# Modulation vectors of a two-layer trunk: VectorE row sums over a transposed w_mod in place of matmuls in the heads

## The reference, cut to what matters

```
def trunk_layer(x, cond, layer, lp, rope, ctx):
    mod = cond @ lp['w_mod'] + lp['b_mod']          # cond (1, 1024), w_mod (1024, 6144)
    sh1, sc1, g1, sh2, sc2, g2 = jnp.split(mod[:, None, :], 6, axis=-1)
    hmix = rmsnorm(x, lp['norm1_g']) * (1 + sc1) + sh1
    mix, new_ctx = token_mixers(hmix, layer, lp, rope, ctx)
    x = x + g1 * mix
    hffn = rmsnorm(x, lp['norm2_g']) * (1 + sc2) + sh2
    gate, up = jnp.split(hffn @ lp['w_ffn_in'], 2, axis=-1)
    x = x + g2 * ((jax.nn.silu(gate) * up) @ lp['w_ffn_out'])
...
        ctx_cond = jax.nn.silu(c_ctx)[None, :]
        lat_cond = jax.nn.silu(c)
```

## Time and profile before

| | |
|---|---|
| three runs | 3978.43, 3982.35, 3986.39 us (median 3982.35) |
| the profiled execution | 3979.51 us; span of its instructions 3977.7 us |
| busy: PE, DVE, POOL, ACT | 86%, 36%, 36%, 21% of the span |
| mean granted TensorE clock | 0.916 of full speed |
| bytes moved | 242.62 MB, mean 61 GB/s |

### The profile page before, as it was taken

How to read it: one execution, slowest core, us unless ns; L and a number is a source line. 1 busy time by engine, 2 the same in 40 slices (tenths; PEclk the granted TensorE clock), 3 DMA queues, 4 the chain that set the end, 5 groups by cost and what they waited for, 6 DMA issues and landing times.

```text
span 3977.7 us, 55062 instructions
## 1 busy us (share of the span) xinstructions
PE 3424.3 (86%) x21792; PEld 3061.2 (77%) x21792; DVE 1432.8 (36%) x2231; ACT 817.8 (21%) x1639; POOL 1437.6 (36%) x1088
## 2 busy tenths in 40 slices
PE   6978887877889987999987888797688998799997
PEld 5967777546569987999977777684384898799996
DVE  2067773355432122111122667705553222211112
ACT  3133332232110112010022333313311111200001
POOL 0454442002215543444424444320040354344443
PEclk8989998877799998999988999997797999899999
DMA  4201112111112211222211111121120121122221
GB/s 163 75 33 43 43 43 75 56 43 51 49 39 75 75 64 53 70 76 70 77 60 58 43 43 45 52 67 44 44 77 28 53 75 64 53 75 69 70 75 69
DMA packets 62882, 242.62 MB, mean 61 GB/s; under 512 B 6961, under 2 KB 6961, under 8 KB 61489
## 3 DMA queue, kind: packets, MB, share of 16 engines
q1 hardware_dynamic: 60336, 224.77, 17.6%
q10 hardware_dynamic: 1728, 12.36, 0.8%
q0 software_dynamic: 576, 2.10, 0.2%
HBM read 234.48 MB, written 4.72 MB: 60 GB/s over the span
## 4 chain that ended last, share of the span: by engine, by line
PE 66%; issue 10%; DVE 9%; POOLq 5%; POOL 4%; ACT 2%; DVEq 2%; DMA 1%; ACTq 0%; SPq 0%
PE ps_G L582 27%; PE ps_GPM L582 26%; POOLq L2002 5%; PE ps_M L960 2%; POOL gu_hi L1985 1%; DVE small L1735 1%; PE ps_GPM L613 1%; PE ps_G L848 1%; POOL gu_lo L1985 1%; POOL big L2011 1%; PE ps_M L905 1%; PE ps_M L662 1%; DVE big L1766 1%; PE ps_M L988 1%; PE ps_M L887 1%
## 5 line engine op out<-in xcount | busy, mean ns | idle before, releaser
L1949 POOL CAST w_hi<-ring 128x1024 fp32r<-128x1024 f32 x296 | 310.1, 1048 | 1596.7 <-PE ps_G L582 983.8
L1951 POOL TENSOR_TENSOR w_lo<-ring,w_hi 128x1024 fp32r<-128x1024 f32 x296 | 740.9, 2503 | 51.8 <-issue 8.9
L582 PE MATMUL ps_G<-room_a,w_hi 128*128 128x320 f32 x1984 | 455.7, 319 | 92.6 <-DVEq L1434 61.9
L582 PE MATMUL ps_GPM<-room_a,w_hi 128*128 128x320 f32 x1984 | 437.5, 309 | 0.0
L582 PEld LDWEIGHTS ps_G<-room_a,w_hi 128*128 128x128 f32 x1984 | 346.4, 196 | 95.8 <-DVEq L1434 63.7
L582 PE MATMUL ps_G<-room_b,w_hi 128*128 128x320 f32 x1408 | 369.0, 315 | 24.0 <-DVEq L1434 24.0
L582 PE MATMUL ps_G<-room_o,w_hi 128*128 128x320 f32 x1280 | 337.4, 313 | 44.3 <-DVEq L1434 44.3
L582 PE MATMUL ps_GPM<-room_b,w_hi 128*128 128x320 f32 x1408 | 361.4, 309 | 0.0
L582 PE MATMUL ps_GPM<-room_o,w_hi 128*128 128x320 f32 x1280 | 332.9, 309 | 0.0
L582 PEld LDWEIGHTS ps_GPM<-room_a,w_hi 128*128 128x128 f32 x1984 | 331.9, 188 | 0.0
L2001 POOL TENSOR_TENSOR outs<-big,con 128x512 f32<-128x512 f32 x168 | 208.7, 1242 | 296.7 <-DVEq L1582 190.5
(11 more groups left out here) (392 smaller groups left out, 5941.4 us busy)
## 6 DMA issues: line engine op xcount, KB each, us to landing
ring<-in_W SPq DMA_DIRECT2D x416, 512.0 KB, 3.5
big<-in_INV ACTq DMA_DIRECT2D x2, 1664.0 KB, 6.8
par<-in_PARAMS ACTq DMA_DIRECT2D x2, 1646.0 KB, 8.9
big<-in_FWD ACTq DMA_DIRECT2D x2, 1632.0 KB, 8.0
x<-in_X SPq DMA_DIRECT2D x1, 2560.0 KB, 8.9
out_Y<-h SPq DMA_DIRECT2D x1, 2560.0 KB, 7.5
con<-in_CONSTS SPq DMA_DIRECT2D x1, 1364.0 KB, 11.7
sc<-in_HYCS ACTq DMA_DIRECT2D x2, 578.5 KB, 3.5
```

Of the source, the lines that this page charges most:

```text
L582: m = pe.matmul(ap, w[wi][:, k, n0:n0 + P], acts[ai][k][:, a:b], start=(k == 0 and i == 0), stop=(k == chunks - 1 and i == 2))
L1949: nc.gpsimd.tensor_copy(hi, raw)
L1951: nc.gpsimd.tensor_tensor(wlo[:, slot * UNIT:(slot + 1) * UNIT], raw, hi.bitcast(F32), ALU.subtract)
```

## The change

The host lays `w_mod` out transposed, as 48 tiles per layer of 128 channels x 1024 inputs (`WMOD`), and both conditions broadcast over the partitions (`COND`, 128x2x1024). ACT applies silu to the broadcast conditions. DVE then makes each tile's 128 channels for both conditions: two `scalar_tensor_tensor` over 128x1024 with a running sum (`accum_out`) along the row, a drain behind each (`mod_tile`). PE's modulation matmuls and turns, ACT's row copies and DVE's bias additions in the heads are gone, and the ring has 304 units in place of 416. Of layer 0, 16 tiles are made ahead of everything else and 32 beside `A`; layer 1's 48 tiles are made beside the `f1` iterations of layer 0's FFN, four or five in each of the 11 iterations. Layer 1 has no next layer, so 96 tiles are made in all.

```diff
+            def mod_tile(w, junk, layer, tile):
+                for q in range(2):
+                    stt(junk, w, 1.0, condv[:, q, :], ALU.mult, ALU.mult, accum_out=modl[:, layer, tile, q:q + 1])
+                    dve.drain()
+            def ring_tiles(tiles_):
+                for r in tiles_:
+                    layer, tile = mod_source(r)
+                    dve.wait_ge(mod_landed[r % MOD_BUFS], 16 * (r // MOD_BUFS + 1))
+                    mod_tile(mod_buffer(r), early_junk if r < EARLY else late_junk, layer, tile)
+                    dve.drain().then_inc(mod_used, 1)
...
-            first_groups, groups = FIRST_MOD // 4, 3 * H
-            for i in range(0, first_groups):
-                add_bias(i + 1, i * 4, cn("b_first")[:, bass.ds(i * 4, 4)])
+            dve.wait_ge(cond_ready, 1)
+            for g in range(4):
+                dve.wait_ge(first_in[g], 16)
+                for t in range(4 * g, 4 * g + 4):
+                    mod_tile(first_tiles[:, t, :], early_junk, 0, t)
...
                 dve.drain().then_inc(g_ready.sem, 1)
+                if L == 0:
+                    ring_tiles(range(EARLY))
+                    add_bias(0, FIRST_TILES, N_MOD, pr("b_mod"))
...
                         I = L * (FT // 2) + i + first // 2
+                        if L == 0:
+                            if I == 0:
+                                dve.wait_ge(cond_ready, 2)
+                            ring_tiles(late_tiles(I))
+                            if I == FT // 2 - 1:
+                                add_bias(1, 0, N_MOD, pr("b_next"))
                         dve.wait_ge(gate_silu, I + 1)
...
             # SP
+            for r in range(EARLY):
+                after.setdefault(2 + r * 13 // EARLY, []).append(r)
+            for i in range(FT // 2):
+                for r in late_tiles(i):
+                    after.setdefault(f1[4 * i + 2], []).append(r)
+            for n in range(DEPTH * UNITS):
+                if n >= RAW:
+                    sp.wait_ge(unit_used, n - RAW + 1)
+                sp.dma_start(rv[:, n % RAW, :], W[n]).then_inc(landed[n % RAW], 16)
...
+                for r in after.get(n, []):
+                    if r >= MOD_BUFS:
+                        sp.wait_ge(mod_used, r - MOD_BUFS + 1)
+                    l, t = mod_source(r)
+                    sp.dma_start(mod_buffer(r), WMOD[l, t]).then_inc(mod_landed[r % MOD_BUFS], 16)
...
             # PE
-                    mod_units("delta", (0, 1, 2, 3), L, hd)
...
-                        if step < 2:
-                            mod_units("delta", (4 + 2 * step, 5 + 2 * step), L, hd)
-                    pe.wait_ge(rows_delta.sem, rows_delta.at(Q, 2))
-                    fill("delta", "cols1", L, hd)
-                    turn_rows(mod_rows)
...
-                        mod_units("attn", (qb,), L, hd)
                         if qb:
                             transposed(qb - 1)
...
             # ACT
+            act.dma_start(par[:, :], PARAMS[0]).then_inc(par_in.sem, 16)
+            condition(1)
```

More of the change, by code:

```diff
@@ L115, in at @@
         bank, base, k, per = self.where[phase, name]
-        ahead = FIRST_FILLS if bank == "GP" else 0
-        return bank, layer * self.total[bank] + step * per + (ahead + base + k + 1)
+        return bank, layer * self.total[bank] + step * per + (base + k + 1)
 def tile_fills(prefix, tiles):
@@ L186 @@
 ]
-FIRST_FILLS = 2 * (FIRST_MOD // 4)
 TURNS = Turns(PLAN)
@@ L200, in at, with trunk_program @@
         return step * self.per + k
-def trunk_program(nc, W, PARAMS, CONSTS, ROPES, HYCS, FWD, INV, X, Y, KNEW, VNEW, SNEW):
+def trunk_program(nc, W, WMOD, COND, PARAMS, CONSTS, ROPES, HYCS, FWD, INV, X, Y, KNEW, VNEW, SNEW):
     ctx = ExitStack()
@@ L420, in trunk_program @@
         consts_in = sem("consts_in")
+        eps_ready = sem("eps_ready")
+        cond_in = sem("cond_in")
         cond_ready = sem("cond_ready")
[L422 to L425, removed]
+        first_in = [sem(f"first_mod_tiles_in_{g}") for g in range(4)]
+        mod_landed = [sem(f"mod_tile_landed_{s}") for s in range(MOD_BUFS)]
+        mod_used = sem("mod_tile_used")
         par_in = sig_("params_in", 16)
@@ L607, in products @@
                     tile_product(phase, f"{prefix}{t}", t, layer, step, w, 0, acts, chunks).then_inc(unit_used, 1)
[L609 to L630, removed]
             def sum_squares(phase, layer, src, k_count, wait):
@@ L1052, in tiles, with condition @@
                 return view[:, bass.ds(at, 1), a:b].rearrange("p a t -> p (a t)")
+            def condition(time):
+                act.wait_ge(cond_in, 16 * time)
+                nc.scalar.activation(condv, condv, ACT.Silu)
+                act.drain().then_inc(cond_ready, 1)
+            act.dma_start(par[:, :], PARAMS[0]).then_inc(par_in.sem, 16)
+            condition(1)
             act.wait_ge(consts_in, 32)
@@ L1058, in _ @@
             act.drain()
[L1059 to L1067, removed]
             def squares(tiles_):
@@ L1436, in _, with add_bias @@
             htiles = [hv[:, k, :] for k in range(KC)]
-            def add_bias(turned, tile, bias):
-                dve.wait_ge(mod_turned, turned)
-                tt(modv[:, bass.ds(tile, 4), :], bank["GP"][:, 0:8].rearrange("p (a b) -> p a b", a=4),
-                   bias.unsqueeze(2).to_broadcast([P, 4, 2]), ALU.add).then_inc(freed["GP"], 1)
+            def mod_tile(w, junk, layer, tile):
[8 more added lines that the diff above has]
+                    dve.drain().then_inc(mod_used, 1)
+            def add_bias(layer, a, b, bias):
+                rows = modl[:, layer, a:b, :]
+                tt(rows, rows, bias[:, a:b].unsqueeze(2).to_broadcast([P, b - a, 2]), ALU.add)
+                dve.drain()
             def tile_product(phase, name, t, layer, step, unit, combine):
@@ L1944, in split @@
                     pool.wait_ge(landed[slot], 16 * (layer * (UNITS // RAW) + step * (len(kinds) // RAW) + (base // RAW + 1)))
-                    pool.wait_ge(unit_used, layer * UNITS + step * len(kinds) + (base - 1))
+                    before = layer * UNITS + step * len(kinds) + (base - 1)
+                    if before > 0:
+                        pool.wait_ge(unit_used, before)
                     hi = whi[:, to * UNIT:(to + 1) * UNIT]
@@ L2220 @@
     arrays = {
-        "W": W, "PARAMS": par, "CONSTS": constants(np.asarray(c), np.asarray(c_ctx), np.asarray(final_g), np.asarray(b_mod[0])),
+        "W": W, "WMOD": wmod, "COND": cond, "PARAMS": par, "CONSTS": constants(np.asarray(final_g)),
         "ROPES": axial_rope(), "HYCS": hyena_constants(), "FWD": fwd, "INV": inv,
```

127 lines of the change are left out of this document (61 added, 66 removed).

## The result

The changed kernel took 4011.03 us in the median of four runs (4003.76 to 4012.55); the kernel before, with a fourth run beside them, 3983.99 us. The ratio is 1.0066 (95% interval 1.0049 to 1.0084): slower by two thirds of a per cent, 3 us from the forecast. The terms of the forecast did worse than its sum. To see that, one compares the start of the same instruction in both traces at the stages' borders.

The account below looks back on a forecast made before the run. PE's GEMM line held over half the chain, so only places where modulation stood in the chain counted. Terms 8 + 26 + 16 - 24 - 9 + 18 = +35 us on 3979.5 gave 4014 us, range 3962 to 4052.

Parts of the forecast that it names:

- One tile, T = 2.8 us: DVE's price for one modulation tile, two running sums over 1024 elements at an estimated 1.30 us each, with gaps.
- Rival 2: The running sum halves DVE's rate, so a tile takes 5.0 us: about 4219 us, chance 0.12.
- DVE stands while POOL splits: A DVE operation with two SBUF inputs does not run during POOL's cast and subtraction: blocked 3.44 us per split.
- Rivals 1 and 3: First: POOL does not block DVE, 3967 us, chance 0.15. Third: only POOL's subtraction blocks, 3984 us, chance 0.15.
- A, +26: A of layer 0 ends at 141.7 us against 115.4, as loads queue behind DVE's 32 tiles: 26 us longer.
- +38: Upper case for A of layer 0: 38 us longer with T = 3.1 us and all 14 splits.
- FFN, +16: FFN of layer 0: four iterations with five tiles make PE wait 5.5 us each, 22 us, taken as 16.
- Start, +8: The first reciprocal, and all of A behind it, moves 8 us later for 16 tiles, waits for loads and two splits.
- -24 for the recursion: DeltaNet heads: 1.3 us won twice a head, plus 0.4 us for turn and bias, 3.0 us over 8 heads.
- +10 for the clock: DeltaNet heads: without the first modulation block PE drops to its lower clock, costing 1.3 us a head.
- Attention heads, -9 and +8: Removing copy and turn wins 1.1 us a head, 9 us over 8 heads; PE's lower clock costs 1 us a head.
- Rival 4: The heads gain nothing, as the clock takes it all and more (+44 in place of +18): 4040 us, chance 0.12.

Follow-up runs that it names:

- e2: Changed kernel with the broadcast conditions copied into four idle PSUM banks for the tiles beside A and the FFN: 3981.95 us, ratio 1.0006 to the kernel before.
- e1: Changed kernel with products of constants on PE where the modulation stood in both kinds of heads: 3973.65 us, ratio 0.9994 to the kernel before.
- e5: Changed kernel with products of constants in the DeltaNet heads alone: 3994.94 us, ratio 1.0042 to the kernel before.
- e6: Changed kernel with products of constants in the attention heads alone: 3986.6 us, ratio 1.0023 to the kernel before.
- e4: Changed kernel with products of constants in both kinds of heads and conditions in PSUM beside A and the FFN: 3951.7 us, ratio 0.9925 to the kernel before.
- e7: As e4, with conditions in PSUM for the first 16 tiles too and the second four tiles loaded ahead of X: 3943.38 us, ratio 0.9916.
- e8: As e7, with 22 more products of constants at the end of each DeltaNet head: 3935.69 us, ratio 0.9897 to the kernel before.

## Why the prediction was right, by its own steps

The direction, the size and the mechanism of the stages with tiles were right; two sets of terms were wrong by about as much in opposite directions.

- *One tile, T = 2.8 us.* In A a tile's two sums, read-outs and gaps took 2.70 us undisturbed (103.67 to 106.37). Rival 2 did not come: the trace shows 1.226 us, so the rule of the Trainium skill's "Vector Engine (DVE) Microarchitecture Reference" on half throughput, in the section on points that are easy to get wrong, does not hold for this form with two f32 inputs in SBUF here (half throughput would have been 2.4 us by the forecast's own working).
- *DVE stands while POOL splits.* Right, and e2 shows the condition: with one input in PSUM the sums (1.22 us) and the splits (1.04 and 2.42 us) overlap at full rate. The size was off: 2.6 us per split, not 3.44. POOL stands too (1.71 and 3.21 us in place of 1.04 and 2.40), so that a DVE operation already running is finished at POOL's cost. Rivals 1 and 3 fall: the cast is drawn out as well, and it draws out the sum beside it.
- *A, +26; measured +21.3.* With 2.70 and 2.6 us and the 13 splits that the trace has ahead of W[15] (12 in the forecast), the forecast's own sum, 5.1 + 29 x 2.70 + 13 x 2.6, puts W[15] at 117.2 us; it was issued at 118.5. One bound beside it was added up wrongly and carried nothing: +38, with T = 3.1 and all 14 splits, is +42 by its own terms (5.1 + 29 x 3.1 + 14 x 3.44 + 14.1 - 115.4).
- *FFN, +16; measured +5.9.* The step that was mis-sized is the iteration with five tiles, put at 5.5 us over. Of the distances between successive L1919 (now L1928) inside a group, three are longer than 28.2 us: 31.7, 30.2 and 30.2, at three of the four iterations with five tiles. The fourth is the first of its group and costs nothing that can be seen (91.2 us from the iteration ahead of it, 92.1 before). The smaller price of a split accounts for most of it, 4 x 0.84 = 3.4 us of the 5.5.
- *Start, +8; measured +5.2.* Both terms, the wait for loads and the two splits, are in the trace.
- *DeltaNet heads, -24 for the recursion and +10 for the clock; measured -2.5.* The -24 is right as a mechanism: from the first L1643 of a head to its last, all eight recursions take 149.8 us before and 129.7 in e1 and e5, -20 where the forecast has 16 x 1.3 = 21, with steps of 5.8 us. The clock's term was mis-sized: the forecast put its cost into the solve's first products alone and left out the recursion, where PE's idle time beside the reciprocal costs 0.8 us (1.42 less 0.61 of wait in the step shown) in step 1 and 0.7 in step 2 on average. In the changed kernel the recursions take 141.2 us, so that 12 of the 20 us are lost there. The rest of the stage is at +6.1 us, close to what the forecast has left for it (+10 for the clock less 0.4 x 8 for turn and bias, +7).
- *Attention heads, -9 and +8; measured +4.6.* The same: the clock took more than the handshakes gave. With products in their place e6 gives -22.2 us, more than the forecast's -9 (-13.0 to -18.9 in the profiled executions of e1, e4, e7 and e8). The products are not shorter than the modulation was (2.1 to 3.5 us per block of eight in a head of e1, 1.9 to 3.6 us before), but the clock over the heads of layer 0 is 0.81 in e1 against 0.75 before. Why it stays higher than with the modulation, and how much of the 22 us that gives, stays open.
- Rival 4 (the clock takes what the heads win) thus held in its mechanism, while its 4040 us also assumed the forecast's sizes for A and the FFN. That the sum came out 3 us from the measured time is in part luck: A, the FFN and the start were put some 18 us too high together, the heads some 17 too low.

## What to carry to other kernels

Work taken off an engine that waits anyway is worth only the places where it stood in the chain, and on TensorE it may also have been what held the clock: look at the granted clock of the stage before counting a gain, and try cheap products in the gap. An idle engine is room only if its new work runs beside that of the others: before placing VectorE work with two SBUF inputs beside GpSimd, look for a row in which the two overlap, and give one input a home in PSUM where banks are idle. A sum of terms that comes out right does not show that the terms are right; compare the traces stage by stage.

## What the runs showed of the hardware that was not expected

- The blocking of DVE and POOL is mutual and also holds for POOL's cast, which reads one tensor: 1.04 us became 1.71 beside a sum. With the second input in PSUM, all 160 sums beside A and the FFN ran between 1.220 and 1.224 us.
- The accumulating form is no slower than the plain one: 1.226 us for 1024 f32 elements, against 1.30 estimated from the plain form's rows, and 0.08 us to read the sum out.
- In the recursion the granted clock left 1.00 (0.81 over 432 to 436 us, 0.66 over 440 to 444) when the modulation no longer filled the gap beside DVE's reciprocal; five products of constants in that gap kept it at 1.00 and DVE's later wait for PE at 0.61 us in place of 1.42.
